# Four blocks of squares added on GpSimd instead of six, four summed by TensorE, at three output products

## The reference

```python
def trunk_layer(...):            # the first part
    ...
    out = merge_branches(...)    # ends in merged @ w_out
    x = x + gate * rmsnorm(out, post_g)

def second_block(...):           # the second part, two layers
    m = attention_mixer(...)     # or recurrent_mixer(...); each ends in ... @ w_out
    x = x + rmsnorm_2(m, norm_mix_post[layer])
    h = rmsnorm_2(x, norm_ffn_pre[layer])
    f = swiglu(h, w_gate, w_up, w_down)
    x = x + rmsnorm_2(f, norm_ffn_post[layer])
```

## Time and profile before

| | |
|---|---|
| median of 3 runs | 1490.91 us (1488.69 to 1491.11) |
| the profiled execution | 1491.8 us, of which its span (first to last instruction) 1490.0 us |
| TensorE busy | 1426.8 us (96%) |
| VectorE, ScalarE busy | 916.6 us (62%), 733.3 us (49%) |
| GpSimd busy | 89.6 us (6%) |
| mean granted TensorE clock | 0.987 |

### The profile page before, as it was taken

How to read it: one execution, slowest core, us unless ns; L and a number is a source line. 1 busy time by engine, 2 the same in 40 slices (tenths; PEclk the granted TensorE clock), 3 DMA queues, 4 the chain that set the end, 5 groups by cost and what they waited for, 6 DMA issues and landing times.

```text
span 1490.0 us, 24078 instructions
## 1 busy us (share of the span) xinstructions
PE 1426.8 (96%) x10000; PEld 1245.5 (84%) x10000; DVE 916.6 (62%) x1536; ACT 733.3 (49%) x1186; POOL 89.6 (6%) x125
## 2 busy tenths in 40 slices
PE   4999999999999998999999989999999989999997
PEld 2666667788887785787899989989999988999997
DVE  4454774445454507686287658877766568967642
ACT  4433332532325335544465655786445468844442
POOL 0100000000000011000000010001221000112200
PEclk9999999999999999999999999999999999999999
DMA  9533231122223272332254565434666725366661
GB/s 310 181 113 113 100 113 58 57 81 76 85 85 113 85 282 103 128 99 72 72 180 147 189 215 184 140 109 162 196 190 223 236 76 182 131 198 190 195 191 48
DMA packets 65243, 212.59 MB, mean 143 GB/s; under 512 B 6704, under 2 KB 16176, under 8 KB 65136
## 3 DMA queue, kind: packets, MB, share of 16 engines
q1 hardware_dynamic: 63808, 205.29, 42.4%
q0 software_dynamic: 1328, 5.77, 1.1%
HBM read 209.98 MB, written 1.05 MB: 142 GB/s over the span
## 4 chain that ended last, share of the span: by engine, by line
PE 86%; DVE 6%; ACT 5%; issue 1%; DMA 1%; SPq 0%; POOL 0%; ACTq 0%; DVEq 0%; POOLq 0%
PE B L687 55%; PE B L1201 7%; PE B L703 5%; PE B L890 3%; ACT WH L1402 2%; DVE WL L2044 2%; PE B L968 1%; PE B L1182 1%; PE B L955 1%; PE B L1212 1%; PE B L715 1%; PE B L839 1%; PE B L840 1%; PE B L1082 1%; PE B L843 1%
## 5 line engine op out<-in xcount | busy, mean ns | idle before, releaser
L2044 DVE TENSOR_TENSOR WL<-RAW,WH 128x1024 fp32r<-128x1024 f32 x336 | 409.0, 1226 | 268.9 <-ACT WH L1402 268.3
L687 PE MATMUL B<-XH,WH 128*128 128x256 f32 (+1 forms) x1584 | 500.6, 316 | 3.1 <-DVE ZG L2200 2.5
L687 PE MATMUL B<-XH,WL 128*128 128x256 f32 (+1 forms) x1584 | 485.2, 306 | 0.0
L687 PE MATMUL B<-XL,WH 128*128 128x256 f32 (+1 forms) x1584 | 484.9, 306 | 0.0
L1402 ACT ACTIVATE WH<-RAW 128x1024 fp32r<-128x1024 f32 x336 | 345.8, 1052 | 107.0 <-DMA RAW<-wstream 106.5
L687 PEld LDWEIGHTS B<-XH,WH 128*128 128x128 f32 x1584 | 298.8, 189 | 30.6 <-issue 7.8
L687 PEld LDWEIGHTS B<-XL,WH 128*128 128x128 f32 x1584 | 298.8, 189 | 21.1 <-issue 6.0
L687 PEld LDWEIGHTS B<-XH,WL 128*128 128x128 f32 x1584 | 298.7, 189 | 16.2
L1201 PE MATMUL B<-HH,WH 128*128 128x256 f32 x304 | 84.3, 277 | 0.0
L1201 PE MATMUL B<-HL,WH 128*128 128x256 f32 x304 | 84.3, 277 | 0.0
L1201 PE MATMUL B<-HH,WL 128*128 128x256 f32 x304 | 84.3, 277 | 0.0
(11 more groups left out here) (353 smaller groups left out, 2534.5 us busy)
## 6 DMA issues: line engine op xcount, KB each, us to landing
RAW<-wstream SPq DMA_DIRECT2D x368, 512.0 KB, 3.6
RAW<-wstream SPq DMA_DIRECT2D x32, 256.0 KB, 6.7
X<-x_t SPq DMA_DIRECT2D x4, 512.0 KB, 7.3
SW<-small POOLq DMA_DIRECT2D x2, 896.0 KB, 10.3
SW<-small POOLq DMA_DIRECT2D x2, 768.0 KB, 8.8
BT<-rel POOLq DMA_DIRECT2D x1, 1024.0 KB, 15.0
X<-consts POOLq DMA_DIRECT2D x1, 768.0 KB, 9.4
out_t<-X SPq DMA_DIRECT2D x3, 256.0 KB, 2.4
```

The source lines that it names most:

```text
L687: last = mm(out, w, x, start=i == 0, stop=i == len(pairs) - 1)
L2044: v.tensor_tensor(lo_of(h), raw_of(h), hi_of(h).bitcast(f32), ALU.subtract).then_inc(lo_ready, 1)
```

## The change

At the three output products with 256 tokens (layer 1 of the first part, attention, recurrence) GpSimd's `post_sum` gets 4 blocks instead of 6, so its add of blocks 4 and 5 (L612) goes. `last_column` sums the blocks 4, 5 and 6 on TensorE where it summed block 6 alone, which are two more plain f32 matmuls of 256 columns at each of the three; with block 7 TensorE then sums four blocks itself. The product with 512 tokens keeps 6, and the two down products have had 4 all along.

```diff
             pool.dma_start(BT[:, :, P:TW], rel_q[:, :, 1, :]).then_inc(bias_in, 16)
-            post_sum(6)
-            post_sum(6)
+            post_sum(4)
+            post_sum(4)
             hidden(0)
             post_sum(4)
-            post_sum(6)
+            post_sum(4)
             hidden(1)
             post_sum(4)
...
                     if kt == KT - 2:
                         sums = take(4, *key)
-                        post_sum_part(sums, w, pb, sq, 6)
+                        post_sum_part(sums, w, pb, sq, 6 if sq is SQ else 4)
```

## The result

| | before | after |
|---|---|---|
| median of the runs | 1491.01 us (20 runs, 1488.69 to 1492.4) | 1492.33 us (20 runs, 1490.81 to 1495.6) |
| ratio, 95% interval | | 1.0013, 1.0007 to 1.0019 |
| the profiled execution | 1491.8 us, span 1490.0 us | 1492.3 us, span 1490.5 us |
| mean granted TensorE clock | 0.987 | 0.987 |

The change costs about 0.1%: 1.3 us by the medians, 1.9 us by the ratio, whose interval goes from 1.0 to 2.8 us. That is inside the 0.2% that I had called no change, and a little above the forecast of 0.84 us.

The account below looks back on a forecast made before the run. TensorE bounds the kernel (86% of the last-ending chain). Place terms +0.86, -0.32 and +0.30 us sum to +0.84 us: 1490.91 + 0.84 = 1491.75 us, range 1489.3 to 1493.9 us.

Parts of the forecast that it names:

- The places: Layer 1, attention and recurrence: each takes 1.65 us between surrounding products, so +0.86, -0.32 and +0.30 us.
- The price of a sum: On TensorE at the three places: each added plain f32 sum of 256 columns costs 0.43 us.
- The bounds of 0.12 and 0.67 us: Per added sum: lower, one fp32r product (whole -1.0 us); upper, a sum starting on an empty pipeline (whole +2.3 us).
- The waits for `PB`: TensorE's waits for GpSimd's partial sum at attention and recurrence both go: -1.18 and -0.56 us.
- The first rival: Attention and recurrence: the stall stays and only the six sums count, +2.6 us, 1493.5 us; chance 7%.
- The added waits for squares at L769: Attention and recurrence: the stall does not move to ScalarE's squares, with margins of 1.3 us and more.
- Whether it reaches the end: Behind all three places the shifts reach the end in full; no wait for a weight piece would swallow them.
- VectorE's freed time: ML subtraction beside GpSimd's third add: about 1.04 us comes back at attention, counted as nothing because VectorE then waits.
- The second rival: Attention and recurrence: VectorE's freed time counts, -1.2 us, 1489.7 us; chance 6%.
- the third rival: Behind layer 1's idle time: one 1.2 GHz TensorE stretch less (-0.7 us, 9%) or more (+2.3 us, 8%).
- the fourth rival: Layer 1's gap and attention's end: two more low-clock stretches, +3.9 us, 1494.8 us; chance 4%.
- sign of being wrong: Places differ from 1.65 us by over 0.1 us, or agree while time behind differs; granted clock behind idle time first suspect.

Follow-up runs that it names:

- Attention alone: Kernel before with only attention's output product changed to four blocks on GpSimd: 1490.73 us against 1490.46 us, ratio 0.9997 (0.9988 to 1.0007).
- layer 1 alone: Kernel before with only the output product of layer 1 of the first part changed to four blocks on GpSimd: one profile, 5.11 instead of 4.24 us there.
- the run with eight more: Kernel before with the sum of PB made nine times instead of once at layer 1's output product: 1494.8 us against 1490.35 us, ratio 1.0028.
- the run with the sums behind: Kernel before, six blocks kept, sums of PB and block 6 behind the next part's first products at attention and recurrence: 1490.61 against 1490.46 us, ratio 0.9997.
- the unused add: Changed kernel with GpSimd still adding blocks 4 and 5, result unused, at attention and recurrence: 5.20 us at attention's place; no whole time given.
- the second one of the changed kernel: Profile of the changed kernel run again without edit: 1492.7 us (11 runs) against 1490.46 us, ratio 1.0004.
- twenty waits more: Kernel before with twenty waits on a long-reached semaphore in TensorE's program behind layer 1: one profile, stretches as before (4.24, 5.51, 4.89, 180.60 us).
- the second: Comparison of the unedited changed kernel, run again, with the kernel before: 1492.7 us (11 runs) against 1490.46 us, ratio 1.0004 (0.9995 to 1.0013).
- eight waits more: Changed kernel with eight waits on a long-reached semaphore in TensorE's program behind layer 1: 180.61 us behind attention; no whole time given.

## Why the prediction was right

**The places.** The forecast was 1.65 us at each, +0.86, -0.32 and +0.30 us. The profiles of the changed kernel show +0.88, -0.33 and +0.29 us, four times over to 0.01 us, together +0.84 us. Attention alone and layer 1 alone gave their own terms. The form at the down product, which had the same instructions without a wait, was the right row to price a new form by.

**The price of a sum.** 0.43 us, in the changed kernel and in the run with eight more (3.46 us). The bounds of 0.12 and 0.67 us were not needed.

**The waits for `PB`.** Both gone, as forecast, with `PB` 3.1 us early at attention. The first rival, that the stall stays, is refuted. The added waits for squares at L769 did not show either.

**Whether it reaches the end.** At layer 1 yes: the time of eight sums more arrived. At attention the stretch behind kept the gain (180.59 us with attention alone changed, 180.60 us before); the time itself is too coarse for 0.3 us. At the recurrence the sum only grew there, so the question did not come up in the change; the run with the sums behind shows that a gain of 0.59 us there was lost to VectorE.

**VectorE's freed time.** Counted as nothing, and so it was; the unused add took it away again and no stretch moved by more than 0.03 us at the places. The second rival is refuted for this change.

**The clock and the rest.** The spans of the two profiles differ by 0.5 us, and not by 0.84, and what lies between is in code that the change does not touch: after came to layer 1's output product 0.5 us earlier, had a faster step ahead of layer 1's last column (-0.52 us) and a slower one behind attention (+0.60 us). One more or one less stretch at the lower clock, the third rival, varies between single executions: in the stretch from 598 to 618 us, which the change does not touch, the granted clock was 1.00 in the profile of before and 0.83 in the second one of the changed kernel, where TensorE did 82 instructions instead of 103. It was 0.83 in the first and fourth of the changed kernel and in the kernel before with twenty waits more, and 1.00 in the third. That agrees with the Trainium skill (TensorE: Matmul & The Clock Gate, Part 1), by which the switching of the clock varies from run to run. Here are the rows, of before and of the second profile of the changed kernel.

```profile
598.00:618.00 20.00, 17.69 (x103) 13.26 (x102) 9.24 (x16) 13.64 (x22) 1.80 (x1) 1.00 0.37 132
```

```profile
598.00:618.00 20.00, 17.69 (x82) 11.41 (x80) 10.11 (x17) 12.70 (x21) 1.80 (x1) 0.83 0.39 131
```

At the places of the fourth rival nothing was added: from 894 to 898 us the granted clock is 0.57 in before and in after, and from 1012 to 1020 us, behind attention, it is 1.00 in both.

**The size.** The first comparison gives 1.0 to 2.8 us, just above 0.84; the second gives -0.7 to +1.9 us, which holds it. The prediction named as a sign of being wrong that the stretches agree and the time behind them does not. Behind attention that happened, by 0.6 us, and its first suspect, the granted clock, was not the cause (1.00 in both rows of those ten microseconds above). This slow step would be worth 0.6 us more if the changed kernel had it always, but it has it in two profiles of four. Whether it has it more often than the kernel before (not in its one profile, nor with eight waits more, and in one of the eight other variants) these runs can't tell. The clock is the other candidate: the mean granted clock is 0.9867 over the 31 runs of the changed kernel in both comparisons and 0.9873 over the 61 of the kernel before in the later ones, on three chips, a difference of two and a half times its standard error. In the changed kernel's 20 runs the time falls by 1.2 us per 0.001 of the mean clock, in the kernel before by 0.5 us. By that 0.0006 would be 0.3 to 0.7 us, an estimate, and no run tests whether the change is its cause. So 0.84 us of the measured 1.3 us are shown by the stretches, and the rest stays open.

## What to carry to other kernels

When work moves from an idle engine onto the bounding one, price it place by place: here the same edit was worth -0.3 us where it ended a wait of 1.2 us and +0.9 us where there was no wait, and even where the wait was 0.56 us it lost 0.3 us, so only the one at attention repays it. Before paying with matmuls for a stall, look for work of the same engine that can stand ahead of it: moving the two sums behind the next part's first products ended the same stalls without a matmul more. And when a stall goes, follow the next engine's queue: VectorE had its cover at attention (1.46 us) and none at the recurrence. Last, set the granted clock of all runs beside their times before a remainder of a microsecond is put down to anything else.

## What the runs showed of the hardware

At the full granted clock (1.00) TensorE has two paces for the same run of `fp32r` products of 256 columns, 0.1133 and 0.1178 us a product, 4% apart. Which of them it takes, and for how long, is not fixed by the program: in unchanged code the stretch from layer 1's first output product to its last column took 19.13 us in ten profiles and 19.65 us in four, and the stretch behind attention 180.60 us in most and 0.6 us more in three of fourteen. In the profile of before the slow one begins at the plain f32 sum of L1170 (1029.3 us) and ends at 1031.3 us. In that of after it begins earlier, at 1023.5 us, behind one step of 0.18 us among the first products behind the norm, and holds on until 1042.3 us. The profile of before has the same single step at 1023.9 us, and the fast pace goes on behind it. No wait is recorded where it ends. Twenty instructions more in TensorE's program left it as it was. What ends it was not found.
